# Rows of unread matmuls on TensorE ahead of nine waits, and two subtractions of VectorE moved up, in a two-block transformer kernel

## The reference, cut

```
for l in range(DEPTH):
    mod = cond @ ada_w[l] + ada_b[l]
    shift, scale, gate = jnp.split(mod, 3, axis=-1)
    h = rms_norm(x, norm_g[l]) * (1.0 + scale[:, None, :]) + shift[:, None, :]
    if l % 2 == 0: z = h @ even_w_in[j] ...   # conv + rwkv7_mix
    else:          z = h @ odd_w_in[j]  ...   # q, k, v, index, gate; dsa_attention
    x = x + gate[:, None, :] * out
...
h = h + moe_swiglu(rms_norm_2(h, ln_ffn[i]), router_w[j], w1[j], w3[j], w2[j])
gate = jax.nn.sigmoid(rms_norm_2(h, ln_ple[i]) @ ple_gate[i])
h = h + gate * (p[i] @ ple_proj[i])
```

## Times and profile before

| | us |
|---|---|
| median of 3 runs | 2052.96 |
| lowest, highest | 2052.47, 2055.84 |
| span of the profiled execution | 2052.6 |

### The profile page before, as it was taken

One profiled execution on the slowest core, in us unless ns is written; L12 is line 12 of the kernel. 1 busy time (PEld: TensorE's weight loads), 2 busy tenths in 40 slices (PEclk: granted clock), 3 DMA queues, 4 the chain that ended last, 5 costly groups with the idle time before them and its releaser, 6 DMA issues. The chain is left out here.

```text
span 2052.6 us, 29833 instructions
## 1 busy us (share of the span) xinstructions
PE 1953.8 (95%) x12519; PEld 1773.6 (86%) x12519; DVE 1426.9 (70%) x1720; ACT 996.0 (49%) x1137; POOL 80.1 (4%) x123
## 2 busy tenths in 40 slices
PE   5988999999998999999999899999999999999998
PEld 4867878878887968999999798989898989898976
DVE  6789996463765346665456488878887888787862
ACT  2511111224366212434355566666666666666654
POOL 3000000000000100100220000000000000000000
PEclk9999999999999999999999999999999999999999
DMA  9845221453432432456753298999898989998970
GB/s 333 267 140 166 85 83 42 156 172 125 143 104 91 158 123 83 145 185 192 211 193 130 95 334 330 342 337 345 333 343 335 341 335 347 333 345 333 342 297 21
DMA packets 225857, 452.29 MB, mean 220 GB/s; under 512 B 6944, under 2 KB 91176, under 8 KB 225720
## 3 DMA queue, kind: packets, MB, share of 16 engines
q1 hardware_dynamic: 222400, 445.44, 61.9%
q0 software_dynamic: 1632, 4.75, 0.8%
q10 hardware_dynamic: 1688, 0.15, 0.1%
HBM read 448.21 MB, written 2.10 MB: 219 GB/s over the span
## 5 line engine op out<-in xcount | busy, mean ns | idle before, releaser
L2002 DVE TENSOR_TENSOR ring_r<-ring,his_r 128x2816 fp32r<-128x2816 f32 (+1 forms) x192 | 586.9, 3085 | 58.4 <-ACT his_r L1543 58.3
L1543 ACT ACTIVATE his_r<-ring 128x2816 fp32r<-128x2816 f32 (+1 forms) x192 | 490.7, 2560 | 193.7 <-DMA ring<-in_moe_w_dram 179.8
L1149 PE MATMUL bank<-his_r,hg_r 128*128 128x352 f32 x2048 | 356.4, 326 | 0.8 <-ACT hg_r L1567 0.8
L1149 PEld LDWEIGHTS bank<-his_r,hg_r 128*128 128x128 f32 x2048 | 334.0, 188 | 1.8 <-issue 0.9
L2475 PE MATMUL bank<-hT,ring 128*128 128x256 f32 x912 | 210.0, 386 | 5.9 <-DVE arena L3053 4.0
L2475 PEld LDWEIGHTS bank<-hT,ring 128*128 128x128 f32 x912 | 171.8, 192 | 33.4 <-issue 10.2
L1149 PE MATMUL bank<-ring_r,hg_r 128*128 128x352 f32 x1024 | 185.9, 323 | 0.0
L1149 PEld LDWEIGHTS bank<-ring_r,hg_r 128*128 128x128 f32 x1024 | 169.0, 188 | 0.0
L3074 DVE SCALAR_TENSOR_TENSOR arena<-ring,cw,arena 128x256 f32<-128x256 f32 x240 | 96.4, 475 | 0.1
L1175 PE MATMUL bank<-his_r,at_hi_r 128*128 128x512 f32 x352 | 93.8, 399 | 0.0
L1175 PE MATMUL bank<-his_r,at_lo_r 128*128 128x512 f32 x352 | 92.5, 396 | 0.0
(11 more groups left out here) (541 smaller groups left out, 2946.1 us busy)
## 6 DMA issues: line engine op xcount, KB each, us to landing
ring<-in_moe_w_dram SPq DMA_DIRECT2D x128, 1408.0 KB, 8.2
ring<-in_moe_w_dram SPq DMA_DIRECT2D x48, 1536.0 KB, 8.7
ring<-in_even_w_in_dram SPq DMA_DIRECT2D x28, 1024.0 KB, 6.5
ring<-in_ffn_w_dram SPq DMA_DIRECT2D x22, 1024.0 KB, 5.3
ring<-in_ada_w_dram SPq DMA_DIRECT2D x20, 1024.0 KB, 10.1
ring<-in_odd_w_in_dram SPq DMA_DIRECT2D x9, 2048.0 KB, 7.8
ring<-in_moe_w_dram SPq DMA_DIRECT2D x16, 1024.0 KB, 6.2
ring<-in_a_w_in_dram SPq DMA_DIRECT2D x6, 2048.0 KB, 8.1
```

Of the source, the lines that this page charges most:

```text
L1149: ins = mm(bank[first + m][:, 0:WC], x[:, KT // 2 * late + k, :], w[:, k, WC * m:WC * m + WC], start=(not late and k == 0 and s == "hg_hi" ...
L1543: A(moe_hi(n), moe_w(n), ACT.Copy).then_inc(sem("moe_hi"), 1)
L2002: V.tensor_tensor(moe_lo(n), moe_w(n), moe_hi(n).bitcast(F32), ALU.subtract).then_inc(sem("moe_lo"), 1)
```

## The change

There are two edits.

First, a new function `keep_busy(b, n)` on PE issues n matmuls of the identity matrix by a matrix of ones (128x128 f32, 128 columns) into bank b, whose content nobody reads. It is called at eleven places, 126 matmuls in all: 22 ahead of `ada(2)` and 6 behind `ada(3)`; 24 behind `z("zR", 4)`; 6 between the two `br_pair(0, ...)`, with a wait for `kar_taken` ahead of them, and 6 ahead of `tok(6)`; 13 ahead of `pe_rest`; 7 in each of the last two blocks of `attend`, with a wait for the last gate tile's copy; 20 behind the router's transposes and 4 behind the ranks; 11 behind `over_rounds`.

Second, DVE makes the low part of the query projection's activations and of its first weights (L1655, L1652) ahead of `modulation(1, 16, 24)`, and no longer behind it.

```diff
@@ pe_rest
-            attend(0, 16, 2, logits, turned, result, lambda b: gate_tile(2 + b) if b < 14 else None)
+            def wait_busy():
+                pe.wait_ge(*took("g", 16))
+                keep_busy(3, 7)
+            attend(0, 16, 2, logits, turned, result, lambda b: gate_tile(2 + b) if b < 14 else wait_busy())
...
             ins.then_inc(sem("router_ready"), 1)
+            keep_busy(5, 20)
             pe.wait_ge(sem("sel_ready"), 1)
...
             mm(bank[1][:, 2 * NE:3 * NE], ones[:, :], SEL[:, 1, :], start=False, stop=True).then_inc(sem("rank_ready"), 1)
+            keep_busy(5, 4)
...
             over_rounds(pe, over, over_expert)
+            keep_busy(0, 11)
             pe_gemm("pp1", lambda k: PPT[2 + k], [(sem("moe_done"), 1)])
@@ dve_rest
             ada(11, 0)
             ada(11, 1)
+            def q_lo(u):
+                dve.wait_ge(sem("q_hi"), u + 2)
+                V.tensor_tensor(q_half(u, ring_r_flat), q_half(u), hb_r[u % 3].bitcast(F32), ALU.subtract).then_inc(sem("q_lo"), 1)
+            dve.wait_ge(sem("q_hi"), 1)
+            V.tensor_tensor(qh_r[:, 1, :, :], hT[:, :, :], qh_r[:, 0, :, :].bitcast(F32), ALU.subtract).then_inc(sem("q_lo"), 1)
+            q_lo(0)
             modulation(1, 16, 24)
...
-            q_lo(0)
             dve.wait_ge(*took("m2", 4))
@@ tensor program
+            def keep_busy(b, n):
+                for _ in range(n):
+                    mm(bank[b][:, 0:P], ident[:, :], ones[:, :], start=True, stop=True)
...
                 norm_tile(0, q)
+            keep_busy(6, 22)
             ada(2)
             ada(3)
+            keep_busy(6, 6)
...
             z("zR", 4)
+            keep_busy(3, 24)
             pe.wait_ge(sem("rwkv_set"), 1)
...
-            for g in (0, 2):
-                br_pair(0, g)
+            br_pair(0, 0)
+            pe.wait_ge(sem("kar_taken"), 8)
+            keep_busy(7, 6)
+            br_pair(0, 2)
             pe.wait_ge(*took("zV", 8))
+            keep_busy(7, 6)
             tok(6)
...
+            keep_busy(6, 13)
+            pe_rest(pe, ada, keep_busy)
```

More of the change, by code:

```diff
@@ L641, in more_pool, with pe_rest @@
             add_up(7)
-        def pe_rest(pe, ada):
+        def pe_rest(pe, ada, keep_busy):
             mm = nc.tensor.matmul
@@ L1648, in dve_rest @@
             step(V.tensor_copy(CHC, POSI[:, :]))
[L1650 to L1655, removed]
             dve.wait_ge(sem("rot_tables"), 4)
@@ L2732, in _ @@
             pe_gemm("eoB", lambda k: YT[:, k, :], [took("eoA", 8)], ready=lambda k: (sem("yb_ready"), k // 4 + 1), between=norm_behind(1, all_of=True))
-            pe_rest(pe, ada)
+            keep_busy(6, 13)
+            pe_rest(pe, ada, keep_busy)
         @block.scalar
```

## The result

| | before | after |
|---|---|---|
| median, us | 2053.86 (4 runs) | 2043.63 (4 runs) |
| lowest, highest | 2052.47, 2055.84 | 2041.01, 2044.39 |
| ratio, 95% interval | | 0.9948, 0.9936 to 0.9959 |
| span of the profiled execution | 2052.6 | 2042.7 |

10.2 us faster where 10.5 was forecast. The sum came out; one of its terms fell well short, and two effects that it did not have, one either way, made up for most of it, as will be seen.

The account below looks back on a forecast made before the run. The prediction took PE, busy for 95% of the span and at times at half clock, as the bound. Won 14.6 less lost 4.1 made net 10.5 us, from the median 2052.96 to 2042.4 us, range 2036.5 to 2047.5.

Parts of the forecast that it names:

- (a): Rows around `ada(2)` and `ada(3)`: the clock often falls again but rises earlier; 1.5 us won, ends 0 and 2.85.
- (b): 24 rows behind `z("zR", 4)`: first `lt_pair`s and the tile behind at full clock; 2.6 us won, ends 1.5 and 3.
- (c): Six and six rows around `br_pair`: the clock may fall again, an earlier rise pays; 2.6 us won, ends 0 and 4.9.
- (d): 13 rows ahead of `pe_rest`: they fit the gap and the tile behind gains; 1.8 us won, ends 1 and 2.
- (g): 20 and 4 rows at the router: rank products and gather run faster; 2.7 us won, ends 2 and 3.
- Rival 2: The clock falls again at (a) and (c), rows there late by what they bring: 2046.5 us, chance 14%.
- Rival 3: DVE, busy from 137 to 200 us, takes back the gains of (a), (b), (c): 2049.1 us, chance 8%.
- Rival 4: Unread rows do not count as work for the clock, so no clock is won: 2060.0 us, chance 4%.
- (e): DVE's two subtractions move into idle time, PE goes on at once behind `ada(11)`; 3.4 us won, ends 2 and 4.
- (f): Seven rows in each of the last two attention blocks: the second seven delay transposes; 1.6 us lost, ends 1 and 2.
- (h): 11 rows behind `over_rounds` cannot fill the gap, push `pp1`: 2.5 us lost, ends 4.9 lost and 2.9 gained.
- Rival 1: The eleven rows behind `over_rounds` do fill the gap and `pp1` runs faster: 2037.0 us, chance 14%.

Follow-up runs that it names:

- experiment 8: The changed kernel measured again, on the chip of experiment 5, experiment 7 and experiment 9: 2043.9 us, ratio 0.9952.
- experiment 2: The changed kernel without the unread rows of the last two attention blocks and the 11 behind `over_rounds`: 2041.22 us, ratio 0.9934.
- experiment 5: The kernel of experiment 2 with ACT's cast `q_cast(2)` moved behind its copy of query tile 0: 2039.47 us, ratio 0.9927.
- experiment 9: The kernel of experiment 5 plus unread rows: 6 between `ada(2)` and `ada(3)`, 5 ahead of `br_pair(0, 0)`, 9 ahead of `br_pair(1, 2)`, 12 at 744 us: 2034.61 us.
- experiment 1: The changed kernel with each of the 126 unread matmuls one column wide in place of 128: 2061.62 us, ratio 1.0044.
- experiment 3: The changed kernel with the 11 unread matmuls ahead of the `over_rounds` branch and not behind it: 2045.77 us, ratio 0.9953.
- experiment 10: The kernel of experiment 9 with 19 more unread rows in and behind the narrow head-weights series near 473 us: 2037.88 us, ratio 0.992.
- 9 again: The kernel of experiment 9 run once more, unchanged: 2033.97 us, ratio 0.9901.
- experiment 6: The kernel before with only ACT's cast `q_cast(2)` moved behind its copy of query tile 0: 2053.67 us, ratio 1.0002.
- experiment 7: The changed kernel with 12 unread rows in place of 24 behind `z("zR", 4)`: 2046.3 us in one run.

## Why the prediction was right, and where it was not

(a), (b), (c), (d), (g): right in mechanism and, in the profiled execution, in size, within 0.4 us each. The forecast for (a) and (c) rested on a second fall of the clock, since one-column matmuls stand there, with only an earlier rise as the gain. The windows at 38.2 and 198.6 show just that: short stretches at 0.50 with the unread rows in them. Rival 2 had the fall at both places right, but not its price: the rows won 1.6 and 3.0 all the same. Where the fall stays away they win more (2.6 at (a) in experiment 8, 4.5 at (c) in experiments 2, 5 and 9), near the upper ends of the forecast. Rival 3 (DVE takes the gains back) didn't come: the lead of 4.1 us at 118 was 4.1 at 196, through the very stretch in which DVE is busiest, and that of 7 us at 226 was still 7 us at 452. Rival 4 would have been experiment 1's kernel, not this one: rows of 128 columns do hold the clock, 1.00 at 109.5 behind 24 of them. The Trainium skill's rule on transposes ("TensorE: Matmul & The Clock Gate", part on PE-mode transpose) does not cover a plain matmul with the identity as an operand: this trace has the clock up behind such rows.

(e): the step that failed is the sentence "PE goes on at once: 3.4 won. Late next is the low part of the second weights ... it hides". PE did go on at once, and the low part did hide. But late next was ACT, whose queue the forecast never walked: it has to copy query tile 0 before PE may write the third tile, and it stood behind a cast and the swaps. The term was 1.5 to 1.9; the rest was there to be had by one moved cast (experiment 5).

(f): right, 1.6 lost; the second seven fill no wait.

(h): right for its reason at the start of `pp1`. The eleven began 2.72 us after the scatter and moved `pp1` by 2.4. Rival 1 fell, and experiment 3 shows that rows ahead of the branch don't fill the gap either. But the term took the delay for the loss: at the full clock PE, without the rows, waits 1.07 us for ACT within `pp1`, so 1.1 is what they cost at its end (experiment 2). It is the same oversight as at (e), the queue of ACT.

What the sum did not have: the new low stretch at 744 (-1.7), and `pp1` at the full clock (+3.0). That the eleven rows earned the 3.0 is not shown. Among the executions without rows there, the clock fell behind the branch in four of seven (before, experiments 9 and 10, and 9 again, but not in 2, 5, 6; in 6 the kernel differs from before by one cast alone). With wide rows behind the branch it fell in one of four (experiment 7), with wide rows ahead of it in the only one (3), with narrow rows too (1). That is too few to tell luck from an effect. What the rows are worth, given what the clock does, is clearer. From the last scatter to the end of `pp1` the lead grows by 0.6 with rows and the full clock and by 1.7 without rows and the full clock; with a fall of 3.4 us it shrinks by 1.0 with rows behind the branch (experiment 7) and grows by 1.5 to 1.6 without. With a fall of 6.8 us and no rows it doesn't move. So the rows pay only if they keep that longest fall away.

The forecast's total was right in part by luck: 3.0 that it had not counted made up for 1.9 at (e) and 1.7 at 744. Its allowance of 1.7 either way for stretches that come or move was needed, and rather small.

## What to carry to other kernels

Unread wide matmuls in a gap of PE pay where PE is the bound, the clock falls behind the gap, and they end before the wait does; each that ends later costs its 0.22 us, and rows that stand where PE doesn't wait, or where it cannot issue, are a loss, less what a later wait for another engine takes up (1.3 of 2.4 us here). When a wait is removed, walk the queue of *every* engine that serves the next few steps, and not only of the engine that was late: the next one may be 1.5 us behind, and one reordered step may free it. And when a low clock moves from one execution to the next, judge an edit by PE's lead at the same instruction, not by the time alone.

## What the runs showed of the hardware

- A matmul of one column in full f32 takes as long as one of 128 (5.72 against 5.52 us for 24), and doesn't hold the clock: 2061.62 against 2043.63 us for the same kernel. The forecast had this from one row of before only.
- The jump on PE over code that isn't run takes 2.6 to 2.9 us, counted from the end of the last matmul ahead of it to the start of the next, whether the one ahead is the scatter or an unread row (2.86, 2.72, 2.70 and 2.60 us in the kernels before and after and experiments 1 and 3). On ACT, DVE and SP the same jump has records of 50 to 72 ns.
- The clock fell at 64.9 us in experiment 5 though PE had not been idle since 40.3 us, the window from 55.0 to 64.8 showing it busy for 9.80 of 9.80 us. What was there were two series of matmuls with 64 rows of weights, a full projection tile between them and one `ada`:

```profile
55.00:64.80 9.80, 9.80 (x49) 8.41 (x49) 6.49 (x11) 6.68 (x16) 0.00 (x0) 1.00 0.86 295
65.00:71.60 6.60, 6.60 (x17) 4.78 (x16) 4.98 (x9) 1.90 (x5) 0.00 (x0) 0.50 1.06 386
```

  It fell near there in experiments 2 and 10 too (65.7, 63.7). The changed kernel runs the same matmuls and kept the clock in both its executions. No run here tells why.
- The same program has its low stretches at different places in different executions: up to 630 us the changed kernel and experiment 2 are one program, with 38, 198, 304, 478, 622 in one and 38, 66, 182, 479, 622 in the other; experiment 8, the changed kernel again, has 177, 198, 304, 478, 621.
